# A four-layer hybrid transformer on one Trainium2 core: the banded attention moved to row and column halves of TensorE, between thirds of the query projections

## What is computed

```python
q, k, v = jnp.split(x @ w_in, [Q_DIM, Q_DIM + N_KV_HEADS * HEAD_DIM], axis=-1)   # 16 query heads, 4 key/value heads of 64
kw, vw = with_prev(k), with_prev(v)              # a block of 128 tokens sees its own block and the one before
sc = jnp.einsum('bqkgd,bskd->bkgqs', qb, kb).astype(jnp.float32) * scale + bias
sc = jnp.where(mb, sc, -jnp.inf)                 # causal, within 128 tokens
m = jnp.maximum(jnp.max(sc, axis=-1, keepdims=True), sink)
p = jnp.exp(sc - m)
p = p / (jnp.sum(p, axis=-1, keepdims=True) + jnp.exp(sink - m))
return jnp.einsum('bkgqs,bskd->bqkgd', p.astype(vb.dtype), vb)     # then @ w_out
```

## Time and profile before

| | |
|---|---|
| median of 3 runs | 2297.75 us |
| profiled execution, first to last instruction | 2298.4 us |
| PE busy | 2234.0 us, 97% |
| ACT busy | 978.7 us, 43% |
| DVE busy | 1208.2 us, 53% |
| POOL busy | 202.8 us, 9% |
| attention units of layer 0, first score matmul to first output projection | 90.27 to 160.45 us |
| the same of layer 3 | 1806.08 to 1877.33 us |

### The profile page before, as it was taken

One profiled execution on the slowest core, in us unless ns is written; L12 is line 12 of the kernel. 1 busy time (PEld: TensorE's weight loads), 2 busy tenths in 40 slices (PEclk: granted clock), 3 DMA queues, 4 the chain that ended last, 5 costly groups with the idle time before them and its releaser, 6 DMA issues.

```text
span 2298.4 us, 33291 instructions
## 1 busy us (share of the span) xinstructions
PE 2234.0 (97%) x11370; PEld 1886.4 (82%) x11370; DVE 1208.2 (53%) x1874; ACT 978.7 (43%) x1711; POOL 202.8 (9%) x158
## 2 busy tenths in 40 slices
PE   7999999999999999999999999999999999999998
PEld 7788888888988888888777788888888888888887
DVE  4565555534365545534496555555335665555534
ACT  3574433324334433434445543333334665333423
POOL 1211000000101000000333110000002211000000
PEclk9999999999999999999999999999999999999999
DMA  4402332332422333332420023333324102323332
GB/s 165 138 19 83 109 92 91 102 106 67 151 89 91 100 101 91 93 108 73 138 74 19 8 76 109 91 95 106 101 82 138 56 26 70 106 94 106 99 96 81
DMA packets 58143, 209.25 MB, mean 91 GB/s; under 512 B 6689, under 2 KB 8913, under 8 KB 57681
## 3 DMA queue, kind: packets, MB, share of 16 engines
q1 hardware_dynamic: 52224, 187.72, 26.1%
q10 hardware_dynamic: 5840, 20.47, 2.5%
HBM read 206.05 MB, written 4.22 MB: 91 GB/s over the span
## 4 chain that ended last, share of the span: by engine, by line
PE 61%; DVE 3%; ACT 3%; issue 2%; POOL 1%; DVEq 0%; DMA 0%; ACTq 0%; POOLq 0%; SPq 0%
PE ps L1121 19%; PE ps L1069 11%; PE ps L1071 11%; PE ps L1070 11%; PE ps L1236 2%; PE ps L1209 1%; PE ps L1080 1%; PE ps L1081 1%; PE ps L1082 1%; POOL w_lo L383 1%; ACT work L454 1%; PE ps L1221 1%; ACT w_hi L420 1%; ACT work L541 1%; DVE act L995 1%
## 5 line engine op out<-in xcount | busy, mean ns | idle before, releaser
L1069 PE MATMUL ps<-h_hi,w_hi 128*128 128x512 f32 x1552 | 604.6, 390 | 0.3 <-POOL w_lo L383 0.3
L1070 PE MATMUL ps<-h_lo,w_hi 128*128 128x512 f32 x1552 | 604.2, 389 | 0.0
L1071 PE MATMUL ps<-h_hi,w_lo 128*128 128x512 f32 x1552 | 604.1, 389 | 0.0
L1023 DVE SCALAR_TENSOR_TENSOR work<-ps,conv_sb,work 128x511 f32<-128x511 f32 (+1 forms) x352 | 247.4, 744 | 445.6 <-ACT work L660 445.4
L719 DVE TENSOR_TENSOR w_lo<-raw,w_hi 128x1024 fp32r<-128x1024 f32 x308 | 378.6, 1230 | 191.5 <-ACT w_hi L420 182.6
L420 ACT ACTIVATE w_hi<-raw 128x1024 fp32r<-128x1024 f32 x352 | 368.3, 1049 | 130.7 <-PE ps L1121 57.5
L660 ACT ACTIVATE work<-ps,conv_sb 128x512 f32<-128x512 f32 x176 | 137.0, 779 | 522.2 <-PE ps L1071 481.4
L1069 PEld LDWEIGHTS ps<-h_hi,w_hi 128*128 128x128 f32 x1552 | 291.5, 188 | 61.1 <-issue 0.6
L1071 PEld LDWEIGHTS ps<-h_hi,w_lo 128*128 128x128 f32 x1552 | 291.4, 188 | 60.3
L1070 PEld LDWEIGHTS ps<-h_lo,w_hi 128*128 128x128 f32 x1552 | 291.5, 188 | 60.2
L383 POOL TENSOR_TENSOR w_lo<-raw,w_hi 128x1024 fp32r<-128x1024 f32 x44 | 117.7, 2682 | 1458.8 <-ACT w_hi L420 1458.8
(11 more groups left out here) (152 smaller groups left out, 2761.6 us busy)
## 6 DMA issues: line engine op xcount, KB each, us to landing
raw<-slabs SPq DMA_DIRECT2D x352, 512.0 KB, 3.5
bias<-bias_dram ACTq DMA_DIRECT2D x3, 2048.0 KB, 10.9
g_post<-gains ACTq DMA_DIRECT2D x8, 512.0 KB, 4.7
g_pre<-gains ACTq DMA_DIRECT2D x7, 512.0 KB, 5.8
x<-x_in SPq DMA_DIRECT2D x4, 512.0 KB, 6.1
bias_dram<-bias_rows ACTq DMA_DIRECT2D x1, 2048.0 KB, 12.5
out<-x ACTq DMA_DIRECT2D x4, 512.0 KB, 2.6
g_pre<-gains SPq DMA_DIRECT2D x1, 512.0 KB, 6.0
```

Of the source, the lines that this page charges most:

```text
L1023: ve.scalar_tensor_tensor(y, ps[:, 2 * par + e, 0:SEQ - sh], conv_sb[:, L, t, tap:tap + 1], y, ALU.mult, ALU.add).then_inc(done, 1)
L1069: pe.matmul(ps[:, bank, :], hi, h_hi[:, k, :], start=k == 0, stop=False)
L1070: pe.matmul(ps[:, bank, :], hi, h_lo[:, k, :], start=False, stop=False)
L1071: last = pe.matmul(ps[:, bank, :], lo, h_hi[:, k, :], start=False, stop=k == KT - 1)
```

## The change

It touches layers 0 and 3 and the making of the bias table.

1. **Scores in row halves.** `q_stage` and POOL's copies go. The queries of a pair's first head lie in partitions 0 to 63 and those of the second in 64 to 127; each head is now a matmul over its own 64 rows of the array, into a PSUM bank of its own (banks 0 and 1, one pair of banks for all units).
2. **Values in column halves.** The 64 columns of values are now the stationary operand and the transposed probabilities move (128 columns); the two heads write partitions 0 to 63 and 64 to 127 of one bank (bank 6). The result comes out transposed, so the scaling, the transpose and the copy of each unit's output go; DVE copies a pair's bank out once in four units (`evac_o`).
3. **Softmax steps merged.** DVE makes bias addition, negation, minimum and the sink's bound in one instruction for each head, with the running minimum as accumulator (`scored`). POOL writes the negated sink as one more column beside the scores, so that ACT's exponentials of 129 or 257 columns give the whole denominator, which they accumulate in PSUM (bank 7). DVE takes its reciprocal, and POOL scales the probabilities before they are transposed (`swa_probs`).
4. **Units between thirds.** A query projection is cut in thirds of 9, 9 and 6 matmuls. The units of pair m stand between the thirds of pair m + 1: in the step of unit u PE issues the transposes of unit u - 2, the values of u - 3, the scores of u, and then a third (blocks 0 to 2; none in block 3). In the last four steps tiles of the output projection stand there instead (`block_of` for token tile 2 and slabs 0 to 3), and the output projection is reordered: token tiles 2, 0, 1, 3 for its first four slabs, then all tiles for the last four.
5. **Bias earlier.** The two small loads for the table stand first in SP's queue, ahead of `x`; the one-hot matmul is PE's first work; ACT stores and spreads the rows within the first norms. The load of the table in layer 0 now comes after the splits of four slabs and ahead of the first `evac_q`.

The loops over units are written out; `down` and `attention` stay as they were for the other layers. Cut to its core:

```diff
+            sp.dma_start(rb_sb[:, :], rel_bias).then_inc(rows_in, 16)
+            sp.dma_start(act[0:BUCKETS, 0, 0:REV], onehot).then_inc(rows_in, 16)
             load_x(0)
             load_x(1)
...
+            def swa_probs(L):
+                s, a = ATT[L] // 2, ATT[L]
+                def sink_column(m, b):
+                    w = len(window(b)) * P
+                    pool.tensor_copy(sw_scored(b)[:, :, w], nsink[:, s, 2 * m:2 * m + 2]).then_inc(sw_sink, 1)
+                pool.wait_ge(nsink_made, 1)
+                pool.wait_ge(q_ev, PAIRS * a + 1)
+                for b in range(TT):
+                    sink_column(0, b)
+                for u in range(UNITS):
+                    m, b = u // TT, u % TT
+                    w = len(window(b)) * P
+                    probs = sw_scored(b)[:, :, 0:w]
+                    pool.wait_ge(sw_recip, UNITS * s + u + 1)
+                    pool.tensor_tensor(probs, probs, rden[:, b, :].unsqueeze(2).to_broadcast([P, 2, w]), ALU.mult)\
+                        .then_inc(sw_norm, 1)
+                    if m + 1 < PAIRS:
+                        sink_column(m + 1, b)
...
-                    order = (root_pre, 0), (root_pre, 1), (split_hi, n), (hi, 0), (split_hi, n + 1), (hi, 1), \
-                            (root_pre, 2), (split_hi, n + 2), (root_pre, 3), (hi, 2), (split_hi, n + 3), (hi, 3)
+                    order = (root_pre, 0), (root_pre, 1), (split_hi, n), (store_rows, 0), (hi, 0), (split_hi, n + 1), (hi, 1), \
+                            (root_pre, 2), (spread_rows, 0), (split_hi, n + 2), (root_pre, 3), (hi, 2), (split_hi, n + 3), (hi, 3)
...
+                def evac_pT(u):
+                    sc.wait_ge(sw_pT, U0 + u + 1)
+                    if u >= 3:
+                        sc.wait_ge(sw_values, U0 + u - 2)
+                    probs = sw_probs_T(u)
+                    sc.activation(probs, ps[:, SW_PT + u % 2, 0:2 * len(window(u % TT)) * P], ACT.Copy).then_inc(sw_pT_ev, 1)
...
+                def exps(u):
+                    b = u % TT
+                    w = len(window(b)) * P + 1
+                    sc.wait_ge(sw_added, U0 + u + 1)
+                    sc.wait_ge(sw_sink, U0 + u + 1)
+                    for e in range(2):
+                        places = sw_scored(b)[:, e, 0:w]
+                        last = sc.activation(places, places, ACT.Exp, bias=negm[:, b, e:e + 1], scale=-1.0,
+                                             accum_out=ps[:, SW_DEN, 2 * b + e:2 * b + e + 1])
+                    last.then_inc(sw_exp, 1)
...
+                if L == 0:
+                    load_bias()
+                evac_q(0)
+                split_hi(nq + AHEAD)
+                for u in range(UNITS):
+                    m, b = u // TT, u % TT
+                    if u >= 2:
+                        evac_pT(u - 2)
+                    if b == 3 and m + 1 < PAIRS:
+                        evac_q(m + 1)
+                    exps(u)
+                    if b == 3 and m + 1 < PAIRS:
+                        split_hi(nq + m + 1 + AHEAD)
+                    if u in (7, 11):
+                        a_part(u // TT - 1)
+                    if u >= 27:
+                        a_part(u - 25)
+                evac_pT(UNITS - 2)
+                evac_pT(UNITS - 1)
+                a_part(PAIRS - 1)
+                for c in range(4):
+                    split_hi(nw + c + AHEAD)
...
+                def scored(u):
+                    m, b = u // TT, u % TT
+                    w = len(window(b)) * P
+                    ve.wait_ge(sw_scores, U0 + u + 1)
+                    if u >= TT:
+                        ve.wait_ge(sw_pT, U0 + u - TT + 1)
+                    for e in range(2):
+                        h = 2 * m + e
+                        last = ve.tensor_tensor_reduce(
+                            sw_scored(b)[:, e, 0:w], ps[:, SW_SCORES + e, 0:w], bias[:, h, 2 * P - w:2 * P],
+                            scale=-1.0, scalar=nsink[:, s, h:h + 1], op0=ALU.add, op1=ALU.min,
+                            accum_out=negm[:, b, e:e + 1])
+                    last.then_inc(sw_added, 1)
...
+                def recip(u):
+                    b = u % TT
+                    ve.wait_ge(sw_exp, U0 + u + 1)
+                    ve.reciprocal(rden[:, b, :], ps[:, SW_DEN, 2 * b:2 * b + 2]).then_inc(sw_recip, 1)
+                def evac_o(m):
+                    ve.wait_ge(sw_values, U0 + TT * m + TT)
+                    ve.tensor_copy(act[:, m, :], ps[:, SW_OUT, :]).then_inc(oT_ev, 1)
...
+                split_lo(nq + AHEAD)
+                ve.wait_ge(nsink_made, 1)
+                ve.wait_ge(bias_ready, BIAS_READY[a])
+                for u in range(UNITS):
+                    m, b = u // TT, u % TT
+                    if u >= 1:
+                        recip(u - 1)
+                    scored(u)
+                    if u >= 6 and b == 2:
+                        evac_o((u - 6) // TT)
+                    if b == 3 and m + 1 < PAIRS:
+                        split_lo(nq + m + 1 + AHEAD)
+                    if u in (8, 12):
+                        a_part(u // TT - 2)
+                    if u >= 28:
+                        a_part(u - 26)
+                recip(UNITS - 1)
+                a_part(6)
+                evac_o(PAIRS - 1)
+                a_part(PAIRS - 1)
+                for c in range(4):
+                    split_lo(nw + c + AHEAD)
...
+                def scores(u):
+                    m, b = u // TT, u % TT
+                    t0, w = window(b)[0], len(window(b)) * P
+                    if u == 0:
+                        pe.wait_ge(kv_ready, s + 1)
+                    if b == 0:
+                        pe.wait_ge(q_ev, PAIRS * a + m + 1)
+                    if u >= 1:
+                        pe.wait_ge(sw_added, U0 + u)
+                    for e in range(2):
+                        rows = slice(HD * e, HD * e + HD)
+                        last = pe.matmul(ps[:, SW_SCORES + e, 0:w], act[rows, Q_AT + m, toks(b)],
+                                         act[rows, K_AT + m // 2, t0 * P:t0 * P + w], start=True, stop=True)
+                    last.then_inc(sw_scores, 1)
+                def transposes_of(u):
+                    b = u % TT
+                    w = len(window(b)) * P
+                    pe.wait_ge(sw_norm, U0 + u + 1)
+                    if u >= 2:
+                        pe.wait_ge(sw_pT_ev, U0 + u - 1)
+                    for e in range(2):
+                        for q in range(w // P):
+                            last = pe.transpose(ps[:, SW_PT + u % 2, e * w + q * P:e * w + (q + 1) * P],
+                                                sw_scored(b)[:, e, toks(q)], ident[:, :])
+                    last.then_inc(sw_pT, 1)
+                def values(u):
+                    m, b = u // TT, u % TT
+                    w, g = len(window(b)) * P, u // TT // 2
+                    pe.wait_ge(sw_pT_ev, U0 + u + 1)
+                    if b == 0 and m:
+                        pe.wait_ge(oT_ev, PAIRS * a + m)
+                    for q, t in enumerate(window(b)):
+                        for e in range(2):
+                            last = pe.matmul(ps[HD * e:HD * e + HD, SW_OUT, toks(b)], vbuf[:, t, HD * g:HD * g + HD],
+                                             sw_probs_T(u)[:, e * w + q * P:e * w + (q + 1) * P],
+                                             start=q == 0, stop=q == len(window(b)) - 1)
+                    last.then_inc(sw_values, 1)
...
+                forward(nq, 0, SW_Q)
+                for u in range(UNITS):
+                    m, b = u // TT, u % TT
+                    if u >= 2:
+                        transposes_of(u - 2)
+                    if u >= 3:
+                        values(u - 3)
+                    scores(u)
+                    if m + 1 < PAIRS and b < 3:
+                        if b == 0 and m >= 1:
+                            pe.wait_ge(q_ev, PAIRS * a + m)
+                        forward(nq + m + 1, 0, SW_Q + (m + 1) % 2, range(3 * b, min(3 * b + 3, KT)))
+                    if m + 1 == PAIRS:
+                        arrived(b)
+                        if b == 0:
+                            pe.wait_ge(q_ev, PAIRS * (a + 1))
+                        block_of(b, 2)
+                for t, stages, free in ((0, ((transposes_of, 30), (values, 29), (transposes_of, 31), (values, 30)),
+                                         (sw_added, UNITS * (s + 1))),
+                                        (1, ((values, 31),), (sw_pT_ev, UNITS * (s + 1))),
+                                        (3, (), (oT_ev, PAIRS * (a + 1)))):
+                    for c in range(4):
+                        for stage, u in stages[c:c + 2] if c % 2 == 0 else ():
+                            stage(u)
+                        if c == 0:
+                            pe.wait_ge(*free)
+                        last = block_of(c, t)
+                        if t == 3:
```

(4 more changed lines are left out.)

300 lines of the change are left out of this document (159 added, 141 removed).

## The result

The changed kernel takes 2314.51 us (median of 5 runs, 2308.70 to 2316.70) beside 2302.25 us for the kernel before on the same chip (median of 5, 2297.45 to 2307.11): ratio 1.005, 95% interval 1.003 to 1.0069. It is slower by half a per cent, just at what the prediction called the limit of telling it from no change. The profiled execution has a span of 2307.0 us; its run took 2308.70, the fastest of the five. Against the span of before that is +8.6.

What follows compares the result with a forecast made beforehand. PE bounds the kernel before; a loop through block 3's chain was expected to bind instead. Layer 0's +11.8 and layer 3's -1.1 give +10.7: 2309.1 us as a span, 2308 as a run; range 2284 to 2326, own range 2302 to 2314.

Steps and rivals of the forecast that it cites:

- The likeliest case: The forecast itself: whole kernel at 2308 us as a run, 2309.1 as a span; chance 0.45.
- the loop: Attention units: block 3's serial chain of 6.2 us plus PE's 8.3 set 14.5 us for four units and a slab.
- the start: Program start: earlier DMA issues cost time, the one-hot matmul leaving PE's path gives 0.9 back; together +0.3 us.
- the slabs: Output projection: slabs 4 to 7 are split late, slab 6 at 8.3 where PE wants 6.8; +1.5 us a layer.
- the clock behind the stall: Layer 0, after PE's wait for the bias: PE runs for a while at granted clock 0.50; +1.5 us.
- Switches: PE changing between full, column and row use: 0.14 to values, 0.2 to scores, 0.2 to projection or transposes; 0.54 a step.
- The rival that they cost nothing: PE's mode switches hide behind the work around them: 12 us a layer faster, 2284 us; chance 0.25.
- Column halves don't overlap: Rival: both heads' values, writing one PSUM bank, run one after the other; 7.5 us a layer more, 2323 us; chance 0.22.
- an estimate of 0.53: Values in column halves: a published speedup scaled to 1.6x gives 0.53 us, not the 0.43 taken; some 2 us a layer more.
- The bias: Layer 0: the table is ready at 60.3 us, so PE stalls behind the first third; +8 us, perhaps 3 more.
- Layer 3: Whole-layer term: 154.0 + 1.5 for late slabs, against 156.6 before; -1.1 us.
- Layer 0: Whole-layer term: 0.5 + 1.5 late slabs + 8 bias wait + 1.5 half clock + 0.3 start; +11.8 us.

Runs made afterwards that it cites:

- four kernels: Changed kernel with bias load ahead of the splits and split's low part behind the reciprocal: both halves 2279.66 us, full-array scores 2291.69, full-array values 2291.94, both full 2297.31.
- the last experiment: Changed kernel with early bias load and later low split, plus output projection slabs 4 and 5 of token tiles 0 and 1 first: 2279.32 us, ratio 0.9902.

## Why the prediction came out as it did

The time, 2314.5, is 6.5 above the forecast of 2308 and inside the range; the profiled execution (2307.0) is 2.1 below the span of the sum (2309.1). The likeliest case is the one that happened. That the span came so close is in part luck, since misses cancel: the loop 5.0 too long and the start 1.1, against 1.6 too little for the slabs, 1.2 for the clock behind the stall, and 1.5 in layer 3's K/V projections that the sum did not have. (The attention stage of layer 0, read as 71.7, goes into its sum as 71.9; that changes nothing.) By its steps:

- **The loop** (14.5 forecast, 14.08 measured). The mechanism was right in every link: scores of block 3, bias, exponentials, both parts of the split, reciprocal, POOL, transposes. The sizes: behind the scores 5.54 against 6.2. The bias step took 0.90 as forecast (an accumulator reading 0.08, the pair of additions 0.41 apart). Both exponentials took 0.92, not 1.1. POOL's scaling of 512 elements took 1.04, not the 1.4 of the straight line between 256 and 1024; this is the largest miss, 0.36. The upper of these two rows is a subtraction with fp32r output, another form, and drew the line too high. PE's part was 8.54 against 8.3. PE's waits, 0.35 and 1.18 against 1 and 1.2: the first is shorter mostly since POOL and the exponentials are faster.
- **Switches** (0.14, 0.2 and 0.2, 0.54 a step): shown at these sizes, 0.21 for the one from values to scores by four kernels and 0.14, 0.20 and 0.20 by the trace's single instructions. The rival that they cost nothing (0.25) asked for rounds 1.4 shorter on PE's side; PE's side was 0.24 longer. It fell. The Trainium skill, TensorEngine Tiling (Array Packing), Key Properties, says that changing the tiling mode drains TensorE, and names no price; the trace agrees that there is one, the 0.14 to 0.20 above.
- **Column halves don't overlap** (0.22): fell on the first row, 0.66 for eight. The Trainium skill, TensorEngine Tiling (Array Packing), Gotcha 1, was carried over in that rival from row tiles to column tiles; the trace shows that it does not carry over here.
  The Trainium skill's figure for three column tiles (TensorE: Matmul & The Clock Gate, "Measured speedup vs the span model"), scaled to two, gave an estimate of 0.53 for eight value matmuls. Start to start the trace shows 0.59 with the switch behind them, 0.89 on full columns, a speedup of 1.5 beside the 1.6 of the estimate.
- **The bias** (+8, and +1.5 for the clock, forecast): the load moved ahead gives 8.1 and 2.7 back in layer 0. The size of the wait was right by two misses that cancel: the table was ready 1.0 later than forecast (a slower landing by 1.6, an earlier issue by 0.6), but the first bias addition could not have started before 53.17, 2.0 later than forecast. The half clock behind it was mis-sized, taken from a shorter stretch.
- **Slabs of the output projection**: waits of 2.1 and 2.5 us in layers 0 and 3, 1.5 forecast. The wait is real, but the last experiment shows that taking it away gives 0.8 at most in a layer, which the medians don't show. As a term of the sum it held for where PE stands, not for what a repair would bring.
- **Layer 3** (-1.1 forecast): -2.9. Six rounds at 0.42 less are 2.5, less 1.0 for the slabs: -2.6 by the corrected terms. The forecast had put 3.1 of the time before on slow us; the trace has 6.8 us at half clock there, 3.4.
- **Layer 0** (+11.8 forecast): +10.1. The same 2.5 less, and 0.6 and 1.2 more for slabs and clock, give 11.1. The start takes off 1.1: it was put at +0.3 and is -0.8. PE's first transposes of the norm start 1.3 later than before (10.70 against 9.37), but the K/V projections don't (26.71 against 26.64), and only the one-hot matmul's 0.8 is left. That gives 10.0.
- **From span to median.** The forecast took 0.65 off its span, since the median of before (2297.75) lies that much below the profiled span. But these are different executions: wherever a run has both numbers, its time is 1.7 above its span (2308.70 and 2307.0). This is 2.3 of the 6.5. The median of the changed kernel is 5.8 higher than its own profiled run, the fastest of five; the span's 2.1 goes the other way, and 0.5 is rounding.

What stays open: why some executions have more half-clock stretches than others of the same program, and what PE work at block 3 alone would give.

## What to carry to other kernels

When work is put between the steps of a pipeline, follow each unit's chain across the engines through their queues: what stood ahead of the reciprocal here was a weight split that nobody was waiting for, and its place cost some 20 us, more than the array halves brought (12 to 18 us). A DMA whose result gates a whole stage is issued before work that only feeds a later one. Using parts of the array pays by the matmul but costs by the switch, so few long stretches in one mode should beat many short ones (no run here tried it); and a wait that vanishes from a profile need not shorten it, if the next stage has its own input late.

## What the hardware showed that was not expected

- Column halves of two heads into one PSUM bank overlap: eight matmuls of 64 stationary and 128 moving columns in 0.66 us, 1.06 with 128 stationary columns.
- The price of a switch falls in part on what follows it: the same full scores of 256 columns took 0.78 from start to start behind column halves and 0.68 behind full values. A switch is 0.09 us and the first weight load, which is no longer hidden: 0.05 with 64 columns, 0.11 with 128.
- In a stall of 8.88 us the clock fell to 1.2 GHz after 4.2 us and stayed there for 5.6 us of work, 2.7 us on top of the stall; without the stall the stretch was gone as well.
- POOL's multiplication of 128x512 took 1.04 us and of 128x256 0.61, so 0.18 fixed and 0.43 for each 256 elements by these two sizes. A straight line to the larger subtraction of the kernel before (2.68 for 1024) had led to expect 1.4.
